# Prompt attention: two turned groups, scores, values of two groups, scores, in place of one group at a time

## The reference, cut to what matters

```python
lg = einsum('bqgjd,bcgd->bgjqc', q, kc) + head_bias(t - cmp_end)
p_cmp = masked_softmax(lg, cmp_end <= t);   o_cmp = p_cmp @ vc
...
p_sel = masked_softmax(lg, s_ok);           o_sel = p_sel @ vs
...
p_win = masked_softmax(lg, w_ok);           o_win = p_win @ vw
o = g0 * o_cmp + g1 * o_sel + g2 * o_win
```

## Time and profile before

| | |
|---|---|
| median of three runs | 3199.96 us (3193.92 to 3200.82) |
| profiled execution, its own time | 3196.87 us |
| its span in the profile | 3195.1 us |
| TensorE busy over the span | 2608.7 us, 82% |
| VectorE, ScalarE, GpSimd busy | 1339.1, 949.9, 727.2 us |
| mean granted clock of TensorE | 0.869 |
| the stage of the change | lines 890 to 1065, from 329.8 to 611.5 us |

### The profile page before, as it was taken

The page is one execution under the profiler, slowest core; times in us unless marked ns, Lnnn a source line. Parts: engine busy times, 40 slices in busy tenths (PEclk is TensorE's granted clock), DMA queues, the critical chain, the costliest instruction groups (busy, mean ns, idle before and its releaser), DMA issues. The chain is left out here.

```text
span 3195.1 us, 41213 instructions
## 1 busy us (share of the span) xinstructions
PE 2608.7 (82%) x16047; PEld 2070.9 (65%) x16047; DVE 1339.1 (42%) x2196; ACT 949.9 (30%) x1279; POOL 727.2 (23%) x546
## 2 busy tenths in 40 slices
PE   8898899699578777399545499999898987999960
PEld 8865566499457767299433388888445536777750
DVE  1033466444273454300576301010233106888858
ACT  1100477522401111201342211111000116777740
POOL 2230255423201222433332311110000251001115
PEclk9998699899767777699656699999897898999985
DMA  4454400211010000211001211110212009999973
GB/s 122 109 162 96 136 2 1 78 44 39 25 39 1 1 1 1 83 40 39 2 2 40 106 40 49 39 44 28 92 73 89 0 2 363 399 388 383 395 293 132
DMA packets 84780, 317.51 MB, mean 99 GB/s; under 512 B 14669, under 2 KB 35805, under 8 KB 63957
## 3 DMA queue, kind: packets, MB, share of 16 engines
q1 hardware_dynamic: 62726, 257.88, 22.6%
q10 hardware_dynamic: 13328, 32.37, 3.0%
q0 software_dynamic: 8608, 25.65, 2.3%
HBM read 281.50 MB, written 38.55 MB: 100 GB/s over the span
## 5 line engine op out<-in xcount | busy, mean ns | idle before, releaser
L2306 DVE TENSOR_TENSOR ex_low<-ex_raw,ex_high 128x2048 fp32r<-128x2048 f32 x138 | 308.7, 2284 | 144.4 <-ACT ex_high L2302 143.7
L2302 ACT ACTIVATE ex_high<-ex_raw 128x2048 fp32r<-128x2048 f32 x138 | 256.2, 1910 | 25.7 <-ACT o L2496 15.4
L172 PE MATMUL ps<-mg_high,mg_wg 128*128 128x344 f32 x576 | 191.0, 332 | 41.5 <-POOL mg_wg L1876 41.5
L174 PE MATMUL ps<-mg_low,mg_wg 128*128 128x344 f32 x576 | 184.4, 320 | 0.0
L173 PE MATMUL ps<-mg_high,mg_wg 128*128 128x344 f32 x576 | 184.3, 320 | 0.0
L1029 POOL TENSOR_SCALAR np_z<-np_z,np_sm 128x640 f32<-128x640 f32 (+12 forms) x128 | 125.5, 1006 | 230.8 <-DVE np_sm L995 230.8
L1894 PE MATMUL ps<-o,mg_wb 128*128 128x344 f32 x576 | 170.4, 452 | 0.0
L172 PE MATMUL ps<-hx_high,hgp_w 128*128 128x344 f32 x384 | 123.7, 322 | 42.4 <-DVE hx_low L164 42.4
L2317 PE MATMUL ps<-ex_high,ex_xh 128*128 128x512 f32 x368 | 150.2, 408 | 8.3 <-DVE ex_xl L2540 8.3
L2318 PE MATMUL ps<-ex_high,ex_xl 128*128 128x512 f32 x368 | 147.1, 400 | 0.0
L2319 PE MATMUL ps<-ex_low,ex_xh 128*128 128x512 f32 x368 | 147.0, 399 | 0.0
(11 more groups left out here) (516 smaller groups left out, 6222.7 us busy)
## 6 DMA issues: line engine op xcount, KB each, us to landing
ex_raw<-in_w_eg SPq DMA_DIRECT2D x46, 1024.0 KB, 7.2
ex_raw<-in_w_eu SPq DMA_DIRECT2D x46, 1024.0 KB, 9.5
ex_raw<-in_w_ed SPq DMA_DIRECT2D x46, 1024.0 KB, 9.7
mg_raw<-in_w_mg SPq DMA_DIRECT2D x24, 512.0 KB, 3.6
scratch_s_rows<-o ACTq DMA_DIRECT2D x23, 512.0 KB, 8.8
dnp_w<-in_w_dn SPq DMA_DIRECT2D x16, 512.0 KB, 3.6
hgp_w<-in_w_hg SPq DMA_DIRECT2D x16, 512.0 KB, 3.5
ns_pg<-in_cache SPq DMA_DIRECT2D x32, 192.0 KB, 2.8
```

The source lines that it names most:

```text
L172: pe.matmul(out, w[:, 0, k, :], x.high[:, k, tokens], start=first, stop=False)
L174: return pe.matmul(out, w[:, 0, k, :], x.low[:, k, tokens], start=False, stop=final)
L2302: act.activation(self.high[:, q], self.raw[:, q], ACT.Copy).then_inc(self.high_done[q], 1)
L2306: eng.tensor_tensor(self.low[:, q], self.raw[:, q], self.high[:, q], ALU.subtract).then_inc(self.low_done[q], 1)
```

## The change

Only the order on two engines and a size change. TensorE counts groups through all the steps and works in pairs: after every second turned group come a place for scores, the values of the two groups that are next (one group behind the turned ones), and another place for scores. A pair can take its second group from the next step. The chunks of an iteration are dealt to its places; if there is none, they all stand at the end. The last values stand after the loop. VectorE takes the output of a step one iteration later than before and as the first entry of `later` rather than the last. The copied blocks have four slots in place of three.

```diff
-    NSL = 3
+    NSL = 4
...
+            units = [(f, u) for f in range(N) for u in range(len(groups(steps[f][0])))]
+            k = 0
             for n in range(N + LAG):
-                pieces = list(range(len(chunks(steps[n][0])))) if n < N else []
-                f = n - LAG
-                units = len(groups(steps[f][0])) + 1 if f >= 0 else 0
-                if f == 0:
+                mine = [("scores", n, m) for m in range(len(chunks(steps[n][0])))] if n < N else []
+                todo = []
+                if n == LAG:
                     pe.wait_ge(s["vtc"], 1)
-                before = spread(pieces, units) if pieces else [[]] * units
-                for u in range(max(units, 1)):
-                    if u < units - 1:
-                        turn(f, u)
-                    if 0 < u < units:
-                        values(f, u - 1)
-                    for m in before[u]:
-                        scores(n, m)
+                for _ in range(len(groups(steps[n - LAG][0])) if n >= LAG else 0):
+                    todo.append(("turn", *units[k]))
+                    if k % 2:
+                        todo += ["gap"] + [("values", *units[v]) for v in (k - 2, k - 1) if v >= 0] + ["gap"]
+                    k += 1
+                gaps = todo.count("gap")
+                parts_of = spread(mine, gaps) if gaps else []
+                at = 0
+                for what in todo or mine:
+                    if what == "gap":
+                        for _, a, m in parts_of[at]:
+                            scores(a, m)
+                        at += 1
+                    elif what[0] == "turn":
+                        turn(*what[1:])
+                    elif what[0] == "values":
+                        values(*what[1:])
+                    else:
+                        scores(*what[1:])
+                if todo and not gaps:
+                    for _, a, m in mine:
+                        scores(a, m)
+            for v in range(len(units) - 1 - len(units) % 2, len(units)):
+                values(*units[v])
...
-            for n in range(N + LAG + 1):
+            for n in range(N + LAG + 2):
...
-                if n > LAG:
-                    later.append(lambda: output(n - LAG - 1))
+                if n > LAG + 1:
+                    later.insert(0, lambda: output(n - LAG - 2))
```

## The result

The changed kernel took 3229.28 us in the median of six runs (3214.32 to 3240.07), the kernel before 3196.94 in its six: ratio 1.0098, 95% interval 1.0065 to 1.0131, 32 us slower. The forecast was 3225, range 3207 to 3240. The profiled execution of the changed kernel took 3240.07 us with a span of 3238.3, so it is 43.2 us over the profiled one of before, and it is the slowest of the six. TensorE's mean granted clock over the span is 0.859 against 0.869.

What follows compares the result with a forecast made beforehand. Prompt attention is bound by TensorE's own in-order list, where an added wait is paid in full. Terms -8.6 + 28.7 + 9.6 + 3.0 + 1.0 - 5.5 = +28.2 us on 3196.87 give 3225, range 3207 to 3240.

Steps and rivals of the forecast that it cites:

- the prediction's own signs of being wrong: Three signs in prompt attention; the one meant here: the clock in 380 to 420 us is not full.
- The other two signs: A second scores chunk starting under 2 us after a 512-column one; turned groups waiting for ScalarE's copies instead.
- (b): TensorE's scores beside scores, 33 joints against 12: each new one waits for VectorE's drain; +28.7 us.
- (f): TensorE waits that go: last scores in iterations 16 to 26, some short ones, tail copies; -5.5 us, 0 to -10.5.
- (c): VectorE's second scaling comes after the third chunk, so the next first turned group waits, iterations 3 to 14; +9.6 us.
- (d): First values of a step wait for the output of two steps earlier, iterations 27 to 31; +3.0 us.
- (a): TensorE's turned groups and values paired: 57 changes of kind saved at 0.15 us; -8.6 us.
- (e): Iterations 17, 19, 21, 23, 25: ScalarE copies the last turned group first, so VectorE drains late; +1.0 us.
- (g): Fourth slot of copied blocks: copies find the values of three units before done anyway; 0 us.
- a rise two or three iterations late: TensorE's full clock delayed by new idle times, held likelier than an eight-iteration delay; 5 to 15 us, within the range.
- the clock rival: Much slower: idle times in iterations 7 to 15 keep TensorE's clock at half; +18 to +40 us on top, chance 0.08.

Runs made afterwards that it cites:

- Experiments 2: The changed kernel with more places for score chunks, so from iteration 6 no two stand side by side; 3205.73 us, ratio 1.0031.
- the second profile: The changed kernel run once more, nothing altered, for another profile; median 3234.8 us, ratio 1.0100.
- version 5: The old order with, in iterations 7 to 15, two score chunks side by side and the second turned group beside the first; 3207.27 us, ratio 1.0028.
- versions 4: The kernel before, with the second score chunk beside the first in iterations 7 to 15, VectorE's list old; 3213.24 us, ratio 1.0061.

## Why the prediction was right

The direction, the size and the mechanism of the waits held. The clock was the weak part: the sum had nothing for it, and one of the prediction's own signs of being wrong appeared, since between 380 and 420 us the clock was not full (0.50 to 416 us). The other two signs did not: a second S starts 2.54 us or more behind a 512-column one, and T waits for the scaling at line 1018 (7.1 us), for ScalarE's copies only 0.4 us, in the tail. The last values end 42.6 us later in the profile (653.8 for 611.2), not 28. The terms one by one:

- (b), scores beside scores, +28.7: the 21 new waits add up to 28.3 us in TensorE's timeline, and 512-column joints take 2.54 to 2.65 us as worked out. The total of the scores' waits rose by 25.5 only, mainly because fifteen short waits of before are gone, 4.1 us in all, for which (f) had 4.5. Experiments 2 and 4 show the joints from both sides.
- (c), the scaling a chunk later, +9.6: 7.1 measured, in ten waits up to 0.8. I counted iterations 3 to 14, but the output enters VectorE's list only in iteration 5: ten, not twelve, in iterations 6 to 15, and at 0.58 to 0.67 rather than 0.80 for the narrow ones.
- (d), values behind the output, +3.0: 3.2 in five waits, 0.65 each where 0.60 was expected.
- (a), joints: 12 and 14 transposes in 1.46 and 1.68 us to the next kind, 0.15 less than apart, as expected; V behind a compressed part starts 0.36 us after it (472.66 to 473.02 above) and saves nothing, as expected. In the tail, 31 to the end, the stage won 3.1 us; I had given it 1.0 in (f) and a part of (a). The 14, from the tail:

```profile
630.75 1.75 PE L915 MATMUL ps<-ident,np_z 128*128 128x128 f32 x14
632.43 0.88 PE L928 MATMUL ps<-np_ptb,np_vt 128*64 128x128 f32 x12
```

- (e), the last copy of the odd iterations, +1.0: no wait of TensorE in iterations 18 to 26 beside the joints shows it; nothing.
- (g), the slot: no wait differs, as expected.
- The clock, left out of the sum and held in the range as a rise two or three iterations late. Iterations 8 to 11 were 19.5 us longer, of which the joints and waits at full clock explain about 7 (4 times 1.21 + 0.7 - 0.15): some 12.5 us are the half clock. The rise came in iteration 11 in place of 7, four iterations late and not eight, so the rival was right in kind and half in size, and the sum lacked it. Together with 4.0 us of a short fall at about 491 us that the second profile has not (41.73 against 37.69 in 16 to 19), it is 16.5 of the 40.9; what is left, 24.4, stands for the sum's 28.2.

That the median came out only 4 us over the forecast is in part luck: the sum was 4 too high apart from the clock, the clock's delay was left to the range, and the profiled execution, in which the terms are read, lies 15 over the forecast. The Trainium skill, "TensorE: Matmul & The Clock Gate", Part 4 (PE-mode transpose), says that the full clock does not engage for transposes, which spoke for the clock rival. That is not what worked here: in version 5, with T beside T and without T's waits, the clock was full by 376 us (1.00 in 376 to 386; one profile), where the kernel before has 0.97.

## What to carry to other kernels

Count the joints that a new order makes as well as those that it takes away: 57 changes of kind at 0.15 us were bought with 21 waits for a drain, 18 of them of 1.25 to 1.55 us, since the banks of both groups of heads are drained before the next chunk may start. When an entry is put at the head of another engine's list of small tasks, look for who waits for the entries that it pushes back. And where TensorE is just reaching its full clock, look at the idle times of an iteration together: here two of them in the new order cost about 12.5 us by the clock and 7 by themselves in iterations 8 to 11, while the joint alone in the old order (versions 4 and 5) left the rise where it was.

## What was not expected of the hardware

In the changed order, with two idle times of 0.65 to 0.74 and 0.99 to 1.26 us in each of the iterations 7 to 11, TensorE stayed at 1.2 GHz until 418 to 421 us, some 43 us longer than before, in three profiles of three. With T's waits taken out it rose at 386 us, with the scores' shortened to 0.3 to 0.6 us before 376, and the same two in the old order gave 391, one profile each; what makes up the rest was not found. Once the clock was full, iterations with two idle times of 1.4 to 1.5 us each kept it, but for falls of some 3 to 10 us in some profiles and not in others.
